# Gate tables of the expert values: one transfer per eight experts cut into four and asked for earlier

## The reference, cut to what matters

```python
def one_block(tb):                                   # tb: 512 tokens x 1024
    q = (tb @ w_query).reshape(-1, PEER_HEADS, 2, PEER_HALF_DIM)
    sc = jnp.einsum('thjd,jkd->thjk', q, sub_keys).astype(jnp.float32)
    ...
    eidx = jnp.take_along_axis(cand_i, pos, axis=-1)
    g = jax.nn.softmax(top_s, axis=-1)
    act = jax.nn.gelu(jnp.einsum('thkd,td->thk', expert_u[eidx], tb), approximate=False)
    wts = (g * act.astype(jnp.float32)).astype(tb.dtype)
    return jnp.einsum('thk,thkd->td', wts, expert_v[eidx])
```

## Time and profile before

| | us |
|---|---|
| three timed runs | 3957.86, 3969.17, 3971.21 |
| their median | 3969.17 |
| span of the profiled execution | 3961.5 |

### The profile page before, as it was taken

The page is one execution under the profiler, slowest core; times in us unless marked ns, Lnnn a source line. Parts: engine busy times, 40 slices in busy tenths (PEclk is TensorE's granted clock), DMA queues, the critical chain, the costliest instruction groups (busy, mean ns, idle before and its releaser), DMA issues. The chain is left out here.

```text
span 3961.5 us, 62211 instructions
## 1 busy us (share of the span) xinstructions
PE 3704.9 (94%) x24967; PEld 3092.5 (78%) x24967; DVE 2528.6 (64%) x4168; ACT 1516.2 (38%) x2134; POOL 1731.1 (44%) x915
## 2 busy tenths in 40 slices
PE   7999997989999999999999699999889998989998
PEld 5777776768888999878777467888778885777887
DVE  6787775776999888588888764566446504533221
ACT  2555554323333555333333333444232224533222
POOL 2333332325666655678888122111234442323443
PEclk9999998999999999999999898999999999999999
DMA  4323334844777888999999143000136532112332
GB/s 175 109 99 101 107 98 164 274 161 162 242 244 244 273 294 298 319 322 345 342 347 338 59 156 127 3 3 14 34 117 219 178 92 86 64 43 91 97 96 89
DMA packets 240338, 656.51 MB, mean 166 GB/s; under 512 B 21432, under 2 KB 106040, under 8 KB 234208
## 3 DMA queue, kind: packets, MB, share of 16 engines
q1 hardware_dynamic: 199776, 493.83, 37.3%
q0 software_dynamic: 36864, 134.23, 9.5%
q10 hardware_dynamic: 3456, 25.17, 1.8%
HBM read 590.15 MB, written 63.00 MB: 165 GB/s over the span
## 5 line engine op out<-in xcount | busy, mean ns | idle before, releaser
L1798 POOL TENSOR_TENSOR peer_wl<-peer_wf,peer_wh 128x1024 fp32r<-128x1024 f32 x272 | 658.6, 2424 | 271.8 <-ACT peer_wh L1816 268.5
L2314 POOL TENSOR_TENSOR ff_wl<-ff_wf,ff_wh 128x1024 fp32r<-128x1024 f32 (+1 forms) x136 | 317.9, 2337 | 452.0 <-ACT ff_wh L2381 452.0
L1816 ACT ACTIVATE peer_wh<-peer_wf 128x1024 fp32r<-128x1024 f32 x272 | 286.9, 1055 | 494.3 <-PE peer_y L1937 215.2
L1935 PE MATMUL peer_y<-peer_xh,peer_wh 128*128 128x384 f32 (+1 forms) x1152 | 402.8, 350 | 30.5 <-ACT peer_aout L1831 14.6
L1937 PE MATMUL peer_y<-peer_xh,peer_wl 128*128 128x384 f32 (+1 forms) x1152 | 395.2, 343 | 0.0
L1936 PE MATMUL peer_y<-peer_xl,peer_wh 128*128 128x384 f32 (+1 forms) x1152 | 394.9, 343 | 0.0
L616 POOL TENSOR_TENSOR br_wl<-br_wf,br_wh 128x1024 fp32r<-128x1024 f32 x80 | 198.0, 2476 | 374.9 <-ACT br_wh L814 374.9
L2381 ACT ACTIVATE ff_wh<-ff_wf 128x1024 fp32r<-128x1024 f32 (+1 forms) x136 | 140.7, 1035 | 521.3 <-PE ff_acc L2343 345.5
L1970 PE MATMUL peer_y<-peer_wh,peer_twh 128*128 128x512 f32 x768 | 304.0, 396 | 27.3 <-DVE peer_twl L2188 26.9
L1972 PE MATMUL peer_y<-peer_wl,peer_twh 128*128 128x512 f32 x768 | 300.7, 391 | 0.0
L1971 PE MATMUL peer_y<-peer_wh,peer_twl 128*128 128x512 f32 x768 | 300.6, 391 | 0.0
(11 more groups left out here) (636 smaller groups left out, 9001.4 us busy)
## 6 DMA issues: line engine op xcount, KB each, us to landing
peer_wf<-in_u SPq DMA_DIRECT2D x128, 512.0 KB
peer_wf<-in_v SPq DMA_DIRECT2D x128, 512.0 KB
ff_wf<-in_w_gu SPq DMA_DIRECT2D x88, 512.0 KB, 3.5
br_wf<-in_w_in SPq DMA_DIRECT2D x80, 512.0 KB, 3.4
mix_aw<-in_w_ada SPq DMA_DIRECT2D x24, 1024.0 KB, 8.4
acts<-peer_aout SPq DMA_DIRECT2D x128, 192.0 KB
gates<-peer_gout SPq DMA_DIRECT2D x12, 2048.0 KB
peer_gout<-acts SPq DMA_DIRECT2D x128, 192.0 KB
```

Source lines behind the costliest of these rows:

```text
L1798: nc.gpsimd.tensor_tensor(wl[:, t % SLOTS], wf[:, t % LOADS], wh[:, t % SLOTS], ALU.subtract).then_inc(w_low, 1)
L1816: nc.scalar.activation(wh[:, t % SLOTS], wf[:, t % LOADS], ACT.Copy).then_inc(w_high, 1)
L1935: nc.tensor.matmul(out, wh[:, slot, k], xh[:, k, 0:n], start=(k == 0), stop=False)
L2314: nc.gpsimd.tensor_tensor(wl[:, u % SLOTS, 0:n], wf[:, u % SLOTS, 0:n], wh[:, u % SLOTS, 0:n], ALU.subtract).then_inc(w_low, 1)
```

## The change

Two things are altered. First, the gates of eight rows no longer come in one transfer of 12 blocks but in four of 3 blocks (384 KB). Part n of the gates of group g + 1 is issued in `load_weights(8g + 3 + n)`, behind its wait for DVE and ahead of its activations. DVE waits for four times as many increments on the same semaphore. Second, the four parts of the gates of group 0 and the activations of row 0 are issued at loop index 142 of the score tiles, those of row 1 at 143 and those of row 2 at 144. What is computed and which bytes are moved stays the same.

```diff
--- before.py
+++ after.py
@@ -1624,6 +1624,8 @@
     GROUPS = DENSE // GROUP
     BLOCKS = DENSE // GATE_BLOCK
     A_RING, G_TILES = 4, 8
+    GATE_PARTS = 4
+    GATE_CUT = BLOCKS // GATE_PARTS
     with Phase(nc, "peer") as ph:
         keys_loaded = ph.sem("keys_loaded")
         loaded = [ph.sem(f"loaded{r}") for r in range(LOADS)]
@@ -1733,16 +1735,18 @@
                     sp.wait_ge(gates_kept, (b + 1) * (GATE_BLOCK // GROUP) + 2)
                     sp.dma_start(io["gates"][b], gout[:, b % 2]).then_inc(gates_stored[b % 2], 16)
 
+                def load_gates(g, n):
+                    blocks = slice(GATE_CUT * n, GATE_CUT * n + GATE_CUT)
+                    sp.dma_start(gin[g % 2][:, blocks], io["gates"][blocks, :, G_TILES * g:G_TILES * g + G_TILES
+                                                                    ].rearrange("b p i t -> p b (i t)")
+                                 ).then_inc(gate_loaded[g % 2], 16)
+
                 def load_weights(e):
-                    if e % G_TILES == 0:
-                        g = e // G_TILES
-                        if g >= 2:
-                            sp.wait_ge(weighted, G_TILES * (g - 1))
-                        sp.dma_start(gin[g % 2], io["gates"][:, :, G_TILES * g:G_TILES * g + G_TILES
-                                                             ].rearrange("b p i t -> p b (i t)")
-                                     ).then_inc(gate_loaded[g % 2], 16)
+                    g, m = divmod(e, G_TILES)
                     if e >= A_RING:
                         sp.wait_ge(weighted, e - A_RING + 1)
+                    if g + 1 < P // G_TILES and A_RING - 1 <= m < A_RING - 1 + GATE_PARTS:
+                        load_gates(g + 1, m - A_RING + 1)
                     sp.wait_ge(act_stored[e % 2], 16 * (e // 2 + 1))
                     sp.dma_start(ain[:, e % A_RING], io["acts"][e]).then_inc(act_loaded[e % A_RING], 16)
 
@@ -1754,15 +1758,20 @@
                     b, m = divmod(t - GATE_AT - LAG, 4)
                     if m == 3 and 0 <= b < BLOCKS:
                         store_gates(b)
+                    if t == SCORE_TILES - 2:
+                        for r in range(2):
+                            sp.wait_ge(gates_stored[r], 16 * (BLOCKS // 2))
+                        for n in range(GATE_PARTS):
+                            load_gates(0, n)
+                        load_weights(0)
+                    if t == SCORE_TILES - 1:
+                        load_weights(1)
                 for t in range(SCORE_TILES, SCORE_TILES + LAG):
                     if t < SCORE_TILES + SLOTS:
                         load(t)
                     store_act(t - LAG)
-                    if t == SCORE_TILES + 1:
-                        for r in range(2):
-                            sp.wait_ge(gates_stored[r], 16 * (BLOCKS // 2))
-                        for e in range(A_RING - 1):
-                            load_weights(e)
+                    if t == SCORE_TILES:
+                        load_weights(2)
                 for e in range(P):
                     if e + A_RING - 1 < P:
                         load_weights(e + A_RING - 1)
@@ -2172,7 +2181,7 @@
 
                 def weights(e):
                     dve.wait_ge(act_loaded[e % A_RING], 16 * (e // A_RING + 1))
-                    dve.wait_ge(gate_loaded[e // G_TILES % 2], 16 * (e // (2 * G_TILES) + 1))
+                    dve.wait_ge(gate_loaded[e // G_TILES % 2], 16 * GATE_PARTS * (e // (2 * G_TILES) + 1))
                     if e >= 2:
                         dve.wait_ge(wt_low, e - 1)
                     split = "p (b t) -> p b t"
```

## The result

| | us |
|---|---|
| before, median of 4 runs | 3970.19 (3957.86 to 3972.27) |
| after, median of 4 runs | 3934.73 (3930.89 to 3940.10) |
| ratio, with its 95% interval | 0.991 (0.9893 to 0.9928) |
| spans of the profiled executions | 3961.5 and 3929.9 |

The changed kernel is faster by 35 us in the medians (29 to 42 by the interval) and by 31.6 us in the spans. The forecast was 3942, 27 us faster.

What follows compares the result with a forecast made beforehand. PE's waits in the value tiles, mainly for DVE at group borders, were taken to lose 40.1 us; 16.4 + 6 + 2.0 + 2.4 = 26.8 us won gave a median of 3942, range 3926 to 3960.

Steps and rivals of the forecast that it cites:

- borders between groups: PE's 19 gaps at 15 borders between groups of eight rows lose 19.3 us; earlier quartered gates win 85%, 16.4 us.
- start: PE's idle and low-clock first value products lose 8.9 us; earlier first gates win 6, bounds 0 and 8.9.
- gap at 1664: PE's gap of 2.01 us at 1664.30, beside POOL catching up; a start without the idle hole removes it, 2.0 us.
- gap at 1768 with its low clock: PE's gap of 2.79 us at 1768.06 and the low clock after it lose 4.8 us; half is won, 2.4.
- gap at 2182: PE's gap of 1.61 us at 2182.33, put down to the end of the gathers, loses 1.9 us; 0 won.
- follow-ups: PE's gaps at 1664.30, 1768.06 and 2182.33, expected to win 2.0, 2.4 and 0 us.
- all is won: Rival: borders, start and the three single gaps are all won, 35 us, median 3934; chance 0.15.
- middle rate: Rival: rows with quarters run near 345 GB/s, so the queue still binds; 10 us won, median 3959; chance 0.14.
- slower rival: Rival: quarters hold up loads of `v` in 60 rows at 332 GB/s; 12 us slower, median 3981; chance 0.06.
- signs of being wrong: Gaps move to quarter rows, their rate is under 353 GB/s, `dot(125)` ends at 1648, or the rest grows.
- what is late next: Start: load of tile 143, then POOL's split, gather of row 125, `dot(125)` and `weights(0)` shift by 3 us.
- the first gates only trade places: Rival: `dot(125)` or tile 143 becomes late instead, start wins nothing; sum 21 us, median 3948; chance 0.15.

Runs made afterwards that it cites:

- e11: Changed kernel plus an unread 384 KB load ahead of the activations in the four rows of eight without a quarter; 3959.36 us, ratio 0.9982 to the kernel before.
- e1: Changed kernel with gates 0 and activations 0 to 2 put back to loop index 145, group quarters kept; 3934.35 us, ratio 0.9919 to the kernel before.
- e2: Changed kernel with the new start kept, later gates whole and in their old place; 3970.52 us, ratio 1.0003 to the kernel before.
- e4: Changed kernel with each later group's four quarters issued back to back in the old place; 3965.83 us, ratio 0.9993 to the kernel before.
- e8: Changed kernel with two gate transfers of 768 KB per group, at rows 3 and 5 of the preceding eight; 3937.70 us, ratio 0.9908 to the kernel before.
- e3: Changed kernel with each later group's gates whole (1536 KB) at row 3 of the preceding eight; 3969.60 us, ratio 1.0006 to the kernel before.

## Why the prediction was right, and where it wasn't

| term | forecast | measured |
|---|---|---|
| borders between groups | 16.4 of 19.3 | 19.3 |
| start | 6.0 of 8.9 | 2.8 |
| gap at 1664 | 2.0 | 2.3 |
| gap at 1768 with its low clock | 2.4 of 4.8 | 4.8 |
| gap at 2182 | 0 | 1.9 |
| new small gaps, and what is spread thin | 0 | -1.4 |
| sum in the stage | 26.8 | 29.7 |

The last column is reckoned as in the prediction. PE took 562.3 us from the last score product to the end of the values before, and takes 526.5 after (1651.11 to 2177.57), 4.3 above the 522.2 of its own work. That is 35.8 won; 6.1 are given back, as the score tiles end at 1651.11 instead of 1645.04. Most of the 4.3, 3.7 by the price of 0.27 more for each, are five gaps of 0.39 to 0.54 between 1655.63 and 1679.32, ahead of rows 1, 3, 4, 5 and 6; before, 2.9 of the loss were spread thin. The other 1.9 up to the span's 31.6 lie outside this stretch and aren't explained.

That the sum came within 3 us is in part luck: the start was 3.2 too high, the borders and follow-ups 7.5 too low, and small gaps of 1.4 were not in it. The rival "all is won" named 3934, the measured median, but its 35 us stand against 29.7 in the stage: the start didn't come in full.

**Right: the view and the place.** The idle time at line 1970 was where the loss sat, and it fell from 27.3 to 2.3 us. The rate was as said (345 to 383 in windows of 34.7 us against "near 350"), and SP's issue of activations is no longer held for 5 us (1.41 at most). The choice between the rates of 332 and 384 decided the sum, and the row with gates in flight was the right one to take. e11 bears it out: the queue gives 386 to 390 when more is asked, so 332 was what the kernel wanted there and not what the queue could do. With this both the middle rate and the slower rival fall: they needed a limit under 353.

Two signs of being wrong did show, and mean little. In the 15 stretches from the issue of a first quarter to 4 us behind that of the last, the rate was 332 to 377 GB/s, in 12 of them under 353; but PE was busy throughout in 14 of them, so this was demand again. The bytes of a quarter are spread over more than its row: the rows between such stretches ran at 350 to 398. So the row that takes 4.27 us because it wants 401 GB/s, from which the term of the borders was worked out, doesn't show. And four of the five small gaps do stand ahead of the rows 3 to 6 of the first group, which carry quarters; e1 carries the same quarters and has none there, so they come with the new start.

**Too careful: the borders and the follow-ups.** I took 85% of the borders for a stretch 0.8 us behind, and all of them went. The 19 gaps stand at 12 of the 15 borders, not at all of them. The gap at 2182.33 I left alone as the gathers' end; it is gone in the changed kernel and in e1, and back in e2 (1.51 us at 2187.57) and e4. It stands ahead of row 122, two rows behind a border, where a product of DVE took 4.43 us beside two subtractions of POOL (2177.38). The one at 1768.06, ahead of row 25, came with the 2.93 us of `peer_wside` told above at e8; e2 has it (2.78 at 1766.41), e1 not. Both are what I had called a catching-up stretch: POOL, held up at the border, subtracts without a pause and DVE's products beside it take long. I had the right price for them and counted half of one; together 4.3 us that the sum lacked.

**Wrong: the start.** The failed step is the one on what is late next. I had the shift of tile 143's issue right (3 us; 3.2 measured) and took the shift of the issue for that of the transfer. ACT could copy it only 6.75 us later than before, behind 1536 KB that had been issued just ahead of it: 8.22 us of ACT's wait. I followed that tile to POOL, the gather and `dot(125)`, and not to ACT, where the eviction of tile 139 is queued behind its copy. So PE lost 3.92 us in the score tiles, in a place that had no gap before, and the low clock that I had counted as gone came there instead. The first value product was forecast for 1646 to 1648 and came at 1650.95. `dot(125)` began at 1644.98 where 1640.39 stood before. The rival "the first gates only trade places" described this in kind. Its price, nothing for the start, misses the measured 2.8 by about as much as my 6.

**Half right: the gap at 1664.** It went, but a start without the idle hole doesn't remove it. It stayed in e1 (1.97 at 1663.88), which has the old start, and in e2 too (1.98 at 1661.60), which has the new one. DVE in e1, then in the changed kernel, at the same place:

```profile
1658.47 2.63 DVE L2185 TENSOR_TENSOR peer_gout<-peer_gout,H 128x384 f32<-128x384 f32 x1
1661.02 2.72 DVE L2194 TENSOR_TENSOR peer_twl<-peer_gout,peer_twh 128x384 fp32r<-128x384 f32 x1
...
1658.74 0.56 DVE L2188 TENSOR_TENSOR peer_gout<-peer_gout,H 128x384 f32<-128x384 f32 x1 [2.12 <-DMA peer_gout<-acts]
1659.21 0.55 DVE L2197 TENSOR_TENSOR peer_twl<-peer_gout,peer_twh 128x384 fp32r<-128x384 f32 x1
```

In e1 both products ran beside subtractions of POOL, and in e2 too (2.61 and 2.72 us). In the changed kernel ACT got the next tile of `v` only at 1660.09, after 4.23 us of waiting, and POOL subtracted from 1661.22 on, when DVE was done. So a late load moved POOL's work away from DVE's there; that was luck and not in the prediction.

**Span and median.** The forecast set the median 7.7 us above the profile's span. The time of one execution lies 2.05 us above its own span here (3931.95 and 3929.9); the rest is where the profiled execution falls in the scatter. After, the median is 4.8 above the profile's span. So 31.6 us in the spans became 35.5 in the medians, and 3 us of the distance to the forecast are this.

## What to carry to other kernels

When a wait names a small transfer, look at what stands ahead of it in the same queue: a burst is harmful by the bytes that are issued in a row, in one piece or in four, so spread it over the steps that precede its use; asking for all of it earlier only moves the wait. Before a burst is moved, follow every load behind it to each engine whose program takes that load ahead of something else, eviction above all, and move it only to where the bytes around it leave room. To know whether a queue limits, compare the rate with what the work asks for at full pace; a rate of 332 GB/s here was demand, and 389 was the limit. And when an engine catches up after a wait, look at what the instructions of the engines beside it cost then.

## What the runs showed of the hardware

- One core's 16 DMA engines gave 388 to 390 GB/s in 12 of 14 windows of 34.7 us, at a share of 1.04 or 1.05, with loads of 192 to 512 KB and gathers mixed (e11). A share of 0.97 to 1.02 was no limit yet: the changed kernel ran so with PE full.
- The issue of a 192 KB load took 4.80 us on SP when 1536 KB had been issued just ahead of it (e3, 1793.71), and it took 1.41 us at most in the 128 issues of the changed kernel, most of them under 0.6.
- A product of DVE with 384 columns took 0.54 to 0.56 us with no subtraction of POOL beside it (118 of them from 1690 us on in the changed kernel), 2.1 us in the median with one beside it (117), and 4.43 and 4.95 us beside two in a row (before, 2177.38 and 1658.74).
- A low clock doesn't follow from a gap's length alone. In e2 the first product after a gap of 2.91 us took 0.50 us, the usual figure for a product behind a gap, and after gaps of 2.78 and 2.47 us 0.79 and 0.80. The granted clock of e2 behind the gaps of 2.91 and of 2.78 us:

```profile
1685.00:1687.00 2.00, 1.81 (x8) 1.51 (x9) 1.33 (x2) 0.65 (x1) 0.00 (x0) 1.00 1.04 404
...
1766.00:1768.00 2.00, 1.58 (x4) 1.29 (x5) 2.00 (x4) 1.40 (x2) 1.24 (x2) 0.50 0.96 309
```

In the changed kernel the 3.92 us at tile 141 were followed by a granted clock of 0.50, that is 1.2 GHz, in the window 1638 to 1640. I can't say from these rows what decides it.
